# Latent attention in a decoder layer: scaled query rows, a maximum written negated, and one reciprocal for four blocks of sums

## The chip, the cores and the metric

The kernel is one program on one core of a Trainium2 chip. The metric is the device time of one execution in microseconds, the median of the runs. Engines are named as the profile names them: PE is TensorE, DVE is VectorE, ACT is ScalarE, POOL is GpSimd, SP is SyncE, which issues DMAs.

## The reference

One decoder layer on 1024 tokens of width 1024, everything in float32: a latent attention (MLA) and a retention side by side, a gated mix of the two, a cross-attention to 256 memory tokens, a gated MLP with a causal convolution, and a final norm. The change lies in the latent attention alone: 8 heads, 96 columns for each query and key (64 plain, 32 rotary), 64 for each value.

```python
q = (rms_norm(c_q, g_q_lat[l]) @ w_uq[l]).reshape(B, S, MLA_HEADS, MLA_NOPE + MLA_ROPE)
q_nope, q_rope = q[..., :MLA_NOPE], rotary(q[..., MLA_NOPE:], positions)
...
o_a = causal_block_attention(q_full, k_full, v_a.transpose(0, 2, 1, 3),
                             (MLA_NOPE + MLA_ROPE) ** -0.5)
...
def one(args):                       # one block of 128 queries
    s = jnp.einsum('bhqd,bhkd->bhqk', q_blk, k).astype(jnp.float32) * scale
    s = jnp.where(kpos[None, :] <= qpos[:, None], s, neg)
    p = jax.nn.softmax(s, axis=-1).astype(v.dtype)
    return jnp.einsum('bhqk,bhkd->bhqd', p, v)
```

## The kernel before

The five engines run streams of their own, written out by hand in one function, and are tied together by counting semaphores only. An engine works through its stream in order: an instruction that waits holds up all that stand behind it on its engine. Products keep float32 accuracy by splitting each operand into a high and a low part and adding three products (`mm3`: high·high, high·low, low·high, lines 336, 341 and 342). So each tile that TensorE reads is made twice: ScalarE copies the high part out of PSUM (line 878), and VectorE subtracts it to get the low part (line 1378, `lo`). Names ending in `h` and `l` are these parts.

The program starts with memory rows, rotary angles and the transposed input. VectorE's first instructions copy constants (line 1386), turn the positions into floats (`posf`, 1387) and multiply them to angles (`ang`, 1401). Behind that come the retention, the gates, the latents, and then the attention.

**The latents.** TensorE sums the squares of the query latents over columns (line 550, semaphore `l_ss`) and those of the key latents (554). ScalarE takes the square root of the first sums into `lrq` (line 1092: 16 columns, two for each of the 8 row tiles) and of the second into `lr` (1095). Before a function that is not loaded, the compiler puts a table load. VectorE inverts `lrq` (1624) and `lr` (1626). The rows of the queries come out of PSUM multiplied by `lrq` into `qrow` (1104).

**The attention.** For each of the 8 heads the 8 blocks of 128 queries are walked in the order 1, 3, 2, 0, 5, 7, 6, 4 (`QORDER`). Block i has (i + 1) · 128 keys, so its rows of scores are 128 to 1024 columns long. I call a block by that number i. Four blocks in a row are a group: 1, 3, 2, 0 fill one half of the output columns, with at most 512 keys, and 5, 7, 6, 4 the other. The code counts the blocks by w (0 to 63) and the groups by g (0 to 15). For a block:

- TensorE makes the scores in PSUM, masks the diagonal block (629) and signals `m_s`. It is two blocks ahead.
- VectorE takes the row maximum into `amax` (1692) and multiplies it by minus the scale into `aneg` (1695), each one column per block, and waits for itself between the two.
- ScalarE takes the exponential of the scale times the score plus `aneg` into `prow` (1149), and with it the sum of the row into one column of `asum`.
- TensorE transposes `prow` in pieces of up to four 128-wide tiles (641); ScalarE and VectorE make `p0h`/`p0l` (first kind of group) or `p1h`/`p1l` (second kind) of them. The pieces alternate between two banks of PSUM, so a transpose waits until the `lo` of the piece two before is done (`m_ptl`).
- VectorE inverts the sum of the row into one column of `ainv` (1711, `m_inv`, semaphore `m_ri`).

Behind a group stand its value matmuls (662: 12 for the first kind, 24 for the second), then TensorE spreads the four columns of `ainv` by transposes against a broadcast (675), ScalarE copies these to `oT` (1133), and VectorE multiplies the value sums by them (1720). Between the blocks of a head the keys and queries of the next head are made (`aux`: transposes of query rows at 607 and key matmuls; the parts are called `kbh`/`kbl` and `mqh`/`mql`). In the last head this is absent, and the splitting of finished outputs (`oth` on ScalarE, `otl` on VectorE) takes its places.

VectorE's order within block w is: the output of the group before last's end (only second block of a group), the low parts of block w, a low part of the next head if one is due, the maximum of block w + 2 and its `aneg`, then the reciprocal of block w + 1. ScalarE's is: the high parts of block w, the exponential of block w + 1, a high part of the next head. TensorE's is: transposes of block w, next head's piece, scores of block w + 2, and behind the first block of a group the value matmuls of the group before.

## Time and profile before

| | us |
|---|---|
| median of 3 runs | 2019.67 (2018.27 to 2021.47) |
| profiled execution, its own time | 2023.43 |
| span in that profile, first to last instruction | 2021.70 |
| mean granted TensorE clock | 0.977 of full speed |
| busy in the span: TensorE / VectorE / GpSimd / ScalarE | 1913.7 / 929.2 / 850.0 / 555.2 |

The profile is one execution taken by the hardware profiler. Times count from the first instruction. [...] The chain of waits goes back from the last instruction, at each step to what released it, or to the instruction before it on its engine; a piece there is only the part of an instruction that lies on the chain. "issue" is time in which the engine waited for nothing that the profile shows. Rows of the instruction timeline give the whole duration, and in brackets the idle time before and what ended it. Small instructions of one engine overlap in these rows, as the next begins while the last one finishes. The attention runs from about 645 to 852 us.

### The profile page before, as it was taken

To read this page: it belongs to the slowest core of one execution; us is meant where nothing else is said; L and a number is where in the kernel's file an instruction comes from. 1 tells how busy PE (TensorE), PEld (TensorE's weight loads), DVE (VectorE), ACT (ScalarE), POOL (GpSimd) and SP (SyncE) were. 2 spreads that over 40 slices of the span, in tenths; PEclk is the share of its full clock that TensorE was granted. 3 is DMA by queue.
4 is the path that set the end of the run, shared out by engine and by line. 5 is a ranking of instruction groups with operands and counts; after the bars stand their busy time and mean duration, and the time that the engine had idled before them with its cause. 6 is when DMAs were issued, how large, how long until landed. Compare 5 with 4: busy or idle time off the path is not lost.

```text
span 2021.7 us, 25216 instructions
## 1 busy us (share of the span) xinstructions
PE 1913.7 (95%) x9196; PEld 1590.4 (79%) x9196; DVE 929.2 (46%) x1518; ACT 555.2 (27%) x976; POOL 850.0 (42%) x324
## 2 busy tenths in 40 slices
PE   7999999999997888889999999999999999999997
PEld 6788888888875777667878878887888788878876
DVE  4345454000116666645345443665157515542664
ACT  6322223100024555531133221322022102210234
POOL 5733333466642000224533334455645565565461
PEclk9999999999987999989999999999999999999998
DMA  6510111223311000143221222111211121112112
GB/s 244 191 42 25 38 31 52 94 94 96 101 32 32 1 1 1 63 165 127 94 73 63 62 75 82 42 52 52 63 53 42 53 71 42 52 53 63 52 52 83
DMA packets 42203, 136.79 MB, mean 68 GB/s; under 512 B 4240, under 2 KB 10512, under 8 KB 41616
## 3 DMA queue, kind: packets, MB, share of 16 engines
q1 hardware_dynamic: 29072, 93.77, 14.8%
q10 hardware_dynamic: 13056, 41.95, 5.5%
q8 instruction: 55, 0.90, 0.2%
q14 instruction: 20, 0.16, 0.0%
HBM read 114.73 MB, written 20.97 MB: 67 GB/s over the span
## 4 chain that ended last, share of the span: by engine, by line
PE 82%; DVE 8%; ACT 4%; issue 2%; DMA 2%; POOL 1%; ACTq 0%; DVEq 0%; SPq 0%; POOLq 0%
PE ps L336 25%; PE ps L341 25%; PE ps L342 25%; PE ps L662 3%; ACT prow L1149 1%; PE ps L641 1%; DVE p1l L1378 1%; DVE t L1381 1%; DVE yb L1902 1%; DMA raw<-in_slabs 1%; DVE amax L1692 1%; PE ps L455 0%; DVE kbl L1378 0%; DVE sab L1755 0%; ACT oT L878 0%
## 5 line engine op out<-in xcount | busy, mean ns | idle before, releaser
L320 POOL TENSOR_SCALAR wh<-raw 128x1024 fp32r<-128x1024 f32 x152 | 428.1, 2816 | 1091.4 <-PE ps L336 905.8
L322 POOL TENSOR_TENSOR wl<-raw,wh 128x1024 fp32r<-128x1024 f32 x152 | 381.2, 2508 | 12.7
L336 PE MATMUL ps<-uh,wh 128*128 128x512 f32 (+1 forms) x576 | 229.5, 398 | 2.4 <-POOL wl L322 2.4
L342 PE MATMUL ps<-uh,wl 128*128 128x512 f32 (+1 forms) x576 | 226.4, 393 | 0.0
L341 PE MATMUL ps<-ul,wh 128*128 128x512 f32 (+1 forms) x576 | 226.2, 393 | 0.0
L336 PE MATMUL ps<-fah,wh 128*128 128x512 f32 x352 | 139.4, 396 | 6.1 <-DVE fal L1378 5.1
L336 PE MATMUL ps<-f0h,wh 128*128 128x512 f32 x352 | 137.0, 389 | 1.3 <-DVE z L1886 1.3
L342 PE MATMUL ps<-fah,wl 128*128 128x512 f32 x352 | 138.0, 392 | 0.0
L341 PE MATMUL ps<-fal,wh 128*128 128x512 f32 x352 | 137.9, 392 | 0.0
L336 PE MATMUL ps<-f1h,wh 128*128 128x512 f32 x352 | 137.1, 390 | 0.3 <-DVE f1l L1381 0.3
L342 PE MATMUL ps<-f1h,wl 128*128 128x512 f32 x352 | 136.9, 389 | 0.0
L341 PE MATMUL ps<-f0l,wh 128*128 128x512 f32 x352 | 136.9, 389 | 0.0
L342 PE MATMUL ps<-f0h,wl 128*128 128x512 f32 x352 | 136.9, 389 | 0.0
L341 PE MATMUL ps<-f1l,wh 128*128 128x512 f32 x352 | 136.9, 389 | 0.0
L336 PEld LDWEIGHTS ps<-uh,wh 128*128 128x128 f32 (+1 forms) x576 | 108.3, 188 | 25.8 <-POOL wl L322 2.6
L342 PEld LDWEIGHTS ps<-uh,wl 128*128 128x128 f32 (+1 forms) x576 | 107.9, 187 | 24.9
L341 PEld LDWEIGHTS ps<-ul,wh 128*128 128x128 f32 (+1 forms) x576 | 108.3, 188 | 23.3
L1333 ACT ACTIVATE ya<-z,sm 128x512 f32<-128x512 f32 x44 | 35.9, 817 | 301.4 <-DVE z L1886 301.4
L1381 DVE SCALAR_TENSOR_TENSOR ya<-z,sm,ya 128x512 f32<-128x512 f32 x88 | 87.9, 999 | 53.8 <-ACT ya L1333 49.9
L1920 DVE TENSOR_TENSOR hF<-ps,hF 128x512 f32 x48 | 33.2, 692 | 144.3 <-PE ps L342 144.0
L1886 DVE TENSOR_TENSOR z<-ps,rbF 128x512 f32<-128x512 f32 x88 | 60.8, 691 | 71.6 <-PE ps L342 67.7
L1608 DVE TENSOR_TENSOR mxr<-ps,sig 128x512 f32<-128x512 f32 x16 | 11.1, 692 | 177.9 <-PE ps L342 177.9
(352 smaller groups left out, 4081.9 us busy)
## 6 DMA issues: line engine op xcount, KB each, us to landing
raw<-in_slabs SPq DMA_DIRECT2D x160, 512.0 KB, 3.6
rawk<-in_slabs SPq DMA_DIRECT2D x4, 1024.0 KB, 9.7
xs<-in_x SPq DMA_DIRECT2D x8, 512.0 KB, 10.5
s_ga<-sig ACTq DMA_DIRECT2D x8, 512.0 KB, 2.6
s_mr<-mxr ACTq DMA_DIRECT2D x8, 512.0 KB, 5.0
xtile<-in_x ACTq DMA_DIRECT2D x8, 512.0 KB, 6.1
sab<-s_ga ACTq DMA_DIRECT2D x8, 512.0 KB, 4.0
mrb<-s_mr ACTq DMA_DIRECT2D x8, 512.0 KB, 5.6
```

The source lines that it names most:

```text
L320: pool.tensor_scalar(wh[:, j, :], raw[:, j % RAWS, :], 1.0, None, ALU.mult).then_inc(S["w_hi"], 1)
L322: pool.tensor_tensor(wl[:, j, :], raw[:, j % RAWS, :], wh[:, j, :].bitcast(f32), ALU.subtract).then_inc(S["w_ready"], 1)
L336: l = pe.matmul(o, lh, rh, start=start, stop=False)
L341: pe.matmul(o, lh, rl, start=False, stop=False)
L342: return pe.matmul(o, ll, rh, start=False, stop=stop)
L641: l = pe.transpose(ps[:, 6 + q % 2, (c % CH) * P:(c % CH + 1) * P], prow[:, w % 2, c * P:(c + 1) * P], ident)
L662: return pe.matmul(ps[:, 1, qs], vv[:, c, v], pp[:, c, qs], start=start, stop=stop, skip_group_check=True)
L1149: act.activation(prow[:, w % 2, 0:n], s2(w)[:, 0:n], ACT.Exp, scale=QK ** -0.5, bias=aneg[:, 0, w % 4:w % 4 + 1], accum_out=asum[:, 0, w % ...
L1333: act.activation(y[:, half(b)], z[:, 2 + b * H2:2 + (b + 1) * H2], ACT.Identity, scale=smc("cw2", c + FB * x_), bias=smc("b_conv", c + FB ...
L1381: return dve.scalar_tensor_tensor(out=o, in0=a, scalar=s_, in1=b_, op0=op0, op1=op1)
L1886: dve.tensor_tensor(z[:, 2 + b * H2:2 + (b + 1) * H2], ps[:, b, :], rbF[:, b, :], ALU.mult).then_inc(d_free[b], 1)
L1920: dve.tensor_tensor(hb, ps[:, b, :], hb, ALU.add).then_inc(d_free[b], 1)
```

## The change

- The query rows carry the scale of the scores. `lrq` is the square root of (sum of squares / 256 + eps); it becomes the square root of 96 times that, by another `scale` and by a bias `epsq` = 96 · eps. Its inverse is the norm's factor times 96^-0.5, and `qrow` is multiplied by it as before. The exponential has no scale any more. `epsq` is a new column, made by VectorE at the start, and ScalarE waits for it before the square root.
- The row maximum goes straight into `aneg`, by a reduction whose result is negated. `amax`, the multiplication and the semaphore `m_mx` between the two are gone.
- The reciprocal is taken once for a group: 128 × 4 instead of four of 128 × 1, behind the maximum that follows the low parts of the group's last block. The sums use both halves of `asum` in turn, so the exponential of the first block of a group waits for the reciprocal of two groups before. TensorE's wait at the transposes of `ainv` counts groups instead of blocks.
- `epsq` takes its column from the padding (80 to 79), so every other tile stays where it was.

```diff
--- before.py
+++ after.py
@@ -148,8 +148,9 @@
         rst_x = sb("rst_x", [P, NT])
         rsm = sb("rsm", [P, NT, 2])
         mst = sb("mst", [P, 3, MB])
+        epsq = sb("epsq", [P, 1])
         amax, aneg, asum, ainv = (sb(n, [P, 2, CH]) for n in ("amax", "aneg", "asum", "ainv"))
-        sb("line_up_tiles", [P, 80])
+        sb("line_up_tiles", [P, 79])
         ps = ctx.enter_context(nc.psum_tensor("ps", [P, 8, H2], f32))
 
 
@@ -256,7 +257,7 @@
                      "r_hi r_lo y_t gn_st var std yn_done yT_t yg_done y_hi y_lo "
                      "g_st0 g_st1 ld_k0 ld_k1 ld_k2 ld_k3 "
                      "l_e l_ss l_std l_rc l_c l_hi l_lo k_row k_r1 k_r2 k_T k_hi k_lo "
-                     "q_r1 q_rope v_evh o_hi o_lo aux_t aux_hi aux_lo m_s m_mx m_neg m_exp m_ptt m_pth m_ptl "
+                     "q_r1 q_rope v_evh o_hi o_lo aux_t aux_hi aux_lo m_s m_neg m_exp m_ptt m_pth m_ptl "
                      "m_pv m_ri sa_ld0 sa_ld1 mr_ld0 mr_ld1 mix_m mix_hi mix_lo "
                      "o_gh o_gl o_sq o_ac o_z ac_h ac_l ss_t ss_s rb_r rb_t rb_c g1_h g1_l h_sp "
                      "xq_h xq_l mm_ld mm_sq mm_st mm_rc mm_n mm_t mm_hi mm_lo kv_h v_done mv_h mv_l kv_sp k_ld v_ld "
@@ -668,7 +669,7 @@
                         one(c, n)
                 one(0, 2, stop=True).then_inc(S["m_pv"], 1)
 
-                pe.wait_ge(S["m_ri"], CH * (g + 1))
+                pe.wait_ge(S["m_ri"], g + 1)
                 pe.wait_ge(S["aux_lo"], USE_OF["sum", g])
                 for j in range(CH):
                     t = UNITS[CH * g + j][1] % CH
@@ -1088,9 +1089,10 @@
                         act.activation(lsq[:, half(b)], ps[:, b, :], ACT.Square).then_inc(d_free[b], 1)
                     else:
                         copy(zkr[:, half(b)], ps[0:ROPE, b, :]).then_inc(d_free[b], 1)
+            act.wait_ge(S["cst"], 5)
             act.wait_ge(S["l_ss"], 1)
             act.activation(lrq[:, :, :], ps[:, 2, 0:2 * NT].rearrange("p (t c) -> p t c", c=2), ACT.Sqrt,
-                           scale=1.0 / QR, bias=cnc("eps")).then_inc(S["l_std"], 1)
+                           scale=float(QK) / QR, bias=epsq[:, :]).then_inc(S["l_std"], 1)
             act.wait_ge(S["l_ss"], 2)
             act.activation(lr[:, :], ps[:, 4:6, :].rearrange("p a n -> p (a n)"), ACT.Sqrt, scale=1.0 / KVR,
                            bias=cnc("eps")).then_inc(S["l_std"], 1)
@@ -1144,10 +1146,13 @@
             def m_exp(w):
                 n = (UNITS[w][1] + 1) * P
                 act.wait_ge(S["m_neg"], w + 1)
+                if w % CH == 0:
+                    at_least(act, S["m_ri"], w // CH - 1)
                 if w >= 2:
                     act.wait_ge(S["m_ptt"], PIECE0[w - 1])
-                act.activation(prow[:, w % 2, 0:n], s2(w)[:, 0:n], ACT.Exp, scale=QK ** -0.5,
-                               bias=aneg[:, 0, w % 4:w % 4 + 1], accum_out=asum[:, 0, w % 4:w % 4 + 1]).then_inc(S["m_exp"], 1)
+                act.activation(prow[:, w % 2, 0:n], s2(w)[:, 0:n], ACT.Exp,
+                               bias=aneg[:, 0, w % 4:w % 4 + 1],
+                               accum_out=asum[:, w // CH % 2, w % CH:w % CH + 1]).then_inc(S["m_exp"], 1)
 
             def m_pth(w):
                 i, g = UNITS[w][1], w // CH
@@ -1385,6 +1390,7 @@
             for o, n in ((ones_r, "ones"), (ident_r, "ident"), (mask_r, "mask")):
                 dve.tensor_copy(o[:, :], cn[:, CN0[n]:CN0[n] + P]).then_inc(S["cst"], 1)
             dve.tensor_copy(posf[:, :], posi[:, :]).then_inc(S["cst"], 1)
+            dve.tensor_scalar(epsq[:, :], cnc("eps"), float(QK), None, ALU.mult).then_inc(S["cst"], 1)
 
             inv = cn[:, CN0["inv"]:CN0["inv"] + NF]
 
@@ -1394,7 +1400,7 @@
             def angle(n):
 
                 if n == 0:
-                    dve.wait_ge(S["cst"], 4)
+                    dve.wait_ge(S["cst"], 5)
                 else:
                     dve.wait_ge(S["angs"], n)
                 if n == 0:
@@ -1688,12 +1694,9 @@
                 n = (UNITS[w][1] + 1) * P
                 c = 2 + 2 * (w % 2)
                 dve.wait_ge(S["m_s"], w + 1)
-                at_least(dve, S["m_exp"], w - 1)
-                dve.tensor_reduce(amax[:, 0, w % 4:w % 4 + 1], ps[:, c:c + 2, :].rearrange("p a n -> p (a n)")[:, 0:n], AX.X,
-                                  ALU.max).then_inc(S["m_mx"], 1)
-                dve.wait_ge(S["m_mx"], w + 1)
-                dve.tensor_scalar(aneg[:, 0, w % 4:w % 4 + 1], amax[:, 0, w % 4:w % 4 + 1], -QK ** -0.5, None, ALU.mult).then_inc(
-                    S["m_neg"], 1)
+                at_least(dve, S["m_exp"], w - 3)
+                dve.tensor_reduce(aneg[:, 0, w % 4:w % 4 + 1], ps[:, c:c + 2, :].rearrange("p a n -> p (a n)")[:, 0:n], AX.X,
+                                  ALU.max, negate=True).then_inc(S["m_neg"], 1)
 
             def m_ptl(w):
                 i, g = UNITS[w][1], w // CH
@@ -1706,10 +1709,9 @@
                        ps[:, 6 + q % 2, 0:(c1 - c0) * P].rearrange("p (a n) -> p a n", n=P),
                        (p1h if g % 2 else p0h)[at]).then_inc(S["m_ptl"], 1)
 
-            def m_inv(w):
-                dve.wait_ge(S["m_exp"], w + 1)
-                dve.reciprocal(ainv[:, w // CH % 2, w % CH:w % CH + 1], asum[:, 0, w % CH:w % CH + 1]).then_inc(
-                    S["m_ri"], 1)
+            def m_inv(g):
+                dve.wait_ge(S["m_exp"], CH * (g + 1))
+                dve.reciprocal(ainv[:, g % 2, :], asum[:, g % 2, :]).then_inc(S["m_ri"], 1)
 
             def m_out(g):
                 h, b = divmod(g, 2)
@@ -1723,7 +1725,6 @@
             NW = len(UNITS)
             m_max(0)
             m_max(1)
-            m_inv(0)
             for w in range(NW):
                 h, r = divmod(w, NT)
                 if w > CH and w % CH == 1:
@@ -1733,8 +1734,8 @@
                     aux_lo(h + 1, AUX_AT[r])
                 if w + 2 < NW:
                     m_max(w + 2)
-                if w + 1 < NW:
-                    m_inv(w + 1)
+                if w % CH == CH - 1:
+                    m_inv(w // CH)
                 if h == MH - 1 and r < 4:
                     o_lo(r // 2, r % 2)
                 if h == MH - 1 and r >= 6:
```

What this does to VectorE around block 5, in the first head. Before: the key part `kbl`, the three small instructions of block 5 (its maximum, `aneg`, the inverse of block 0), the low part of block 0 (`p0l`), the next `kbl`, and the same for block 7.

```order
L1378 TENSOR_TENSOR kbl<-ps,kbh 64x512
L1692 TENSOR_REDUCE amax<-ps 128x1
L1695 TENSOR_SCALAR aneg<-amax 128x1
L1711 RECIPROCAL ainv<-asum 128x1
L1378 TENSOR_TENSOR p0l<-ps,p0h 128x128
L1378 TENSOR_TENSOR kbl<-ps,kbh 64x512
L1692 TENSOR_REDUCE amax<-ps 128x1
L1695 TENSOR_SCALAR aneg<-amax 128x1
L1711 RECIPROCAL ainv<-asum 128x1
L1378 TENSOR_TENSOR p1l<-ps,p1h 128x4x128
```

The same place in the changed kernel, from the same `kbl` to block 5's first `p1l`.

```order
L1383 TENSOR_TENSOR kbl<-ps,kbh 64x512
L1698 TENSOR_REDUCE aneg<-ps 128x1
L1383 TENSOR_TENSOR p0l<-ps,p0h 128x128
L1383 TENSOR_TENSOR kbl<-ps,kbh 64x512
L1698 TENSOR_REDUCE aneg<-ps 128x1
L1714 RECIPROCAL ainv<-asum 128x4
L1383 TENSOR_TENSOR p1l<-ps,p1h 128x4x128
```

Block 5's maximum is now followed at once by `p0l`, and block 7's by the reciprocal of the whole first group.

VectorE at the end of a head, from the last query part `mql` on: the maximum of the next head's block 1, the low parts of block 4 (`p1l`, two pieces), the maximum of the next head's block 3, the low part of its block 1 (`p0l`). Before:

```order
L1378 TENSOR_TENSOR mql<-ps,mqh 96x512
L1692 TENSOR_REDUCE amax<-ps 128x1
L1695 TENSOR_SCALAR aneg<-amax 128x1
L1711 RECIPROCAL ainv<-asum 128x1
L1378 TENSOR_TENSOR p1l<-ps,p1h 128x4x128
L1378 TENSOR_TENSOR p1l<-ps,p1h 128x128
L1692 TENSOR_REDUCE amax<-ps 128x1
L1695 TENSOR_SCALAR aneg<-amax 128x1
L1711 RECIPROCAL ainv<-asum 128x1
L1378 TENSOR_TENSOR p0l<-ps,p0h 128x2x128
```

And in the changed kernel:

```order
L1383 TENSOR_TENSOR mql<-ps,mqh 96x512
L1698 TENSOR_REDUCE aneg<-ps 128x1
L1383 TENSOR_TENSOR p1l<-ps,p1h 128x4x128
L1383 TENSOR_TENSOR p1l<-ps,p1h 128x128
L1698 TENSOR_REDUCE aneg<-ps 128x1
L1714 RECIPROCAL ainv<-asum 128x4
L1383 TENSOR_TENSOR p0l<-ps,p0h 128x2x128
```

Nothing stands between the first maximum and `p1l` any more.

ScalarE at the square root of the query latents, with what each instruction waits for. `zkr` is the last copy of the latents, and the table load brings the square root. Before:

```order
L878 ACTIVATE zkr<-ps 32x512 [waits done0]
L878 ACTIVATE zkr<-ps 32x512 [waits done1]
L1092 ACT_TABLE_LOAD
L1092 ACTIVATE lrq<-ps,cn 128x16 [waits l_ss]
L1095 ACTIVATE lr<-ps,cn 128x1024 [waits l_ss]
L878 ACTIVATE qrow<-ps,lrq 128x384 [waits done0,l_rc]
```

And in the changed kernel:

```order
L879 ACTIVATE zkr<-ps 32x512 [waits done0]
L879 ACTIVATE zkr<-ps 32x512 [waits done1]
L1094 ACT_TABLE_LOAD [waits l_ss]
L1094 ACTIVATE lrq<-ps,epsq 128x16 [waits cst]
L1097 ACTIVATE lr<-ps,cn 128x1024 [waits l_ss]
L879 ACTIVATE qrow<-ps,lrq 128x384 [waits done0,l_rc]
```

The root now has two waits, and the one for TensorE's sums (`l_ss`) stands ahead of the table load, which waited for nothing before.

## Rows read from the trace of the kernel before

**Rows 1.** The page: shares of the chain that ended last, by engine.
```profile
PE 82%; DVE 8%; ACT 4%; issue 2%; DMA 2%; POOL 1%; ACTq 0%; DVEq 0%; SPq 0%; POOLq 0%
```

**Rows 2.** The attention: length, busy PE, PEld, DVE, ACT, POOL; clock, DMA share, GB/s.
```profile
645.00:852.00 207.00, 175.99 (x1058) 147.65 (x1057) 137.52 (x336) 117.79 (x274) 10.27 (x4) 0.97 0.03 7
```

**Rows 3.** The instructions of lines 1695 and 1711: ns min/median/max, first and last start.
```profile
L1695 DVE TENSOR_SCALAR aneg<-amax x64: 153/154/155, 644.9 to 847.0; 128x1 f32<-128x1 f32 x64
L1711 DVE RECIPROCAL ainv<-asum x64: 151/153/164, 646.4 to 848.8; 128x1 f32<-128x1 f32 x64
```

**Rows 4.** Waits in the attention, 645 to 852: us in total, times, longest.
```profile
PE ps L641 <- DVE p1l L1378: 18.7, 23, 1.6
...
ACT prow L1149 <- DVE aneg L1695: 13.2, 22, 0.9
```

**Rows 5.** The chain through one head, 697 to 724: start us, us, what.
```profile
697.01 4.65 PE ps L662 x24
...
706.56 0.95 DVE amax L1692
...
707.53 0.17 DVE aneg L1695
...
707.72 0.99 ACT prow L1149 x2
...
721.00 0.42 DVE amax L1692
...
721.45 0.08 DVE aneg L1695
721.53 0.14 DVE ainv L1711
721.67 0.60 DVE p1l L1378
```

**Rows 6.** The chain in the other heads: first and last of each place.
```profile
655.29 0.16 DVE aneg L1695
...
668.91 0.15 DVE ainv L1711
...
826.21 0.14 DVE ainv L1711
...
837.72 0.17 DVE aneg L1695
```

**Rows 7.** Timeline of that head: PE at `kbl`, then DVE and ACT around `p1l`.
```profile
709.97 0.64 PE L607 MATMUL ps<-cn,qrow 128*96 128x128 f32 x4 [0.20 <-DVE kbl L1378]
...
720.39 0.69 DVE L1378 TENSOR_TENSOR mql<-ps,mqh 96x512 fp32r<-96x512 f32 x1 [0.48 <-ACT mqh L878]
...
721.59 0.67 DVE L1378 TENSOR_TENSOR p1l<-ps,p1h 128x512 fp32r<-128x512 f32 x1
...
721.64 0.47 ACT L1149 ACTIVATE prow<-ps,aneg 128x256 f32<-128x256 f32 x1 [0.18 <-DVE aneg L1695]
```

**Rows 8.** Timeline of the last head: `oth` on ACT, `otl` on DVE.
```profile
834.82 0.63 ACT L878 ACTIVATE oth<-oT 128x512 fp32r<-128x512 f32 x1
...
835.62 0.68 DVE L1378 TENSOR_TENSOR otl<-oT,oth 128x512 fp32r<-128x512 f32 x1
```

**Rows 9.** Timeline of ACT at the square roots of the latents.
```profile
591.51 1.28 ACT L1092 ACT_TABLE_LOAD   x1
595.29 0.27 ACT L1092 ACTIVATE lrq<-ps,cn 128x16 f32<-128x16 f32 x1 [2.50 <-PE ps L550]
598.91 1.11 ACT L1095 ACTIVATE lr<-ps,cn 128x1024 f32<-128x1024 f32 x1 [3.35 <-PE ps L554]
```

**Rows 10.** Timeline of DVE at the start.
```profile
7.78 0.83 DVE L1401 TENSOR_TENSOR ang<-posf,cn 128x640 f32<-128x640 f32 x1
```

**Rows 11.** Behind the last block: the window 850 to 855, then the chain.
```profile
850.00:855.00 5.00, 3.66 (x9) 2.92 (x10) 1.52 (x4) 1.05 (x3) 0.00 (x0) 0.50 0.76 279
...
851.34 7.08 PE ps L662 x24
```

## The prediction

> **What bounds the kernel now.** I read the page first. Of the chain that ended last TensorE has 82%, VectorE 8%, ScalarE 4% [rows 1]. So VectorE and ScalarE matter only where TensorE waits for them. The change touches the causal attention of the eight heads, which runs from about 645 us to 852 us. There TensorE is busy for 176.0 of 207.0 us, VectorE for 137.5, ScalarE for 117.8 [rows 2]: no engine is full, and the time is set by a chain that goes from one engine to the next. One head takes some 26 us.
>
> The three instructions that the change is about are, for each of the 64 query blocks, the row maximum, its product with minus the scale (154 ns) and one reciprocal (153 ns) [rows 3]. Added up the last two are 64 × 0.154 + 64 × 0.153 = 19.6 us of VectorE. The waits in this stretch show ScalarE waiting for `aneg` 22 times, 13.2 us, and TensorE waiting for VectorE's `p1l` 23 times, 18.7 us [rows 4]. Neither figure is a gain: each is the whole wait, of which the small instructions are the last part. What counts is where they lie on the chain.
>
> The chain through one head [rows 5] goes: the 24 value matmuls of the head before (4.65 us); copies; the maximum of block 5 on VectorE (0.95), then `aneg` (0.17 beside 0.02 of issue), then block 5's exponential. From there a key copy leads to TensorE, whose scores and value matmuls run without a gap. It comes back to VectorE with the maximum of the next head's block 1 (0.42), then `aneg` (0.08) and `ainv` (0.14), then `p1l` of block 4, which frees the PSUM bank that TensorE's next transposes need. Those lead straight into the next 24 value matmuls. So of eight `aneg` and eight `ainv` in a head, two and one are on the chain. The other heads repeat it: block 5's `aneg` is on the chain 8 times, once a head from 655.29 to 837.72, and the pair before `p1l` 7 times, with `ainv` from 668.91 to 826.21 [rows 6].
>
> **The change, part by part.**
>
> *`aneg` of block 5 goes.* The maximum ends at 707.51 and the exponential starts at 707.72 [rows 5]. With the maximum written negated the exponential can start 0.02 us after it: 0.19 us earlier, 8 times, 1.52 us. Next late is the key copy behind it, `kbl` and TensorE's transposes of the queries, and these move by the same 0.19, since TensorE waits 0.20 us for that `kbl` [rows 7].
>
> *`aneg` and `ainv` of the next block 1 go.* The maximum ends at 721.42 [rows 5], `p1l` starts at 721.59 [rows 7]. Two VectorE instructions without a wait between them overlap by 0.08: `mql` runs 720.39 to 721.08 [rows 7], the maximum starts at 721.00. So `p1l` could start at 721.34, 0.25 earlier. The exponential of block 1 must be there as well: it waited 0.18 us for `aneg` [rows 7], gains that, and then its ScalarE predecessor is what is late. Gain for TensorE between 0.18 and 0.25; I take 0.25, also what the chain counts (721.42 to 721.67), since in the chain `p1l` comes last. Seven times: 1.75 us (bounds 1.3 to 1.8). [...]
>
> *The last head* has no next head to prepare. `otl` stands there between `ainv` and block 2's `p0l`. It starts at 835.62 behind `ainv` and needs `oth`, which ends at 834.82 + 0.63 = 835.45 [rows 8]; so it gains about 0.14, and half of that is lost again, because `p0l` then waits for its copy. I take 0.07 (bounds 0 and 0.25) on top of the 0.19 of `aneg` already counted.
>
> *The reciprocals, one of 4 columns for every four blocks.* 64 become 16. They wait for the last exponential of the group, which is done when they are reached, as `p1l`/`p0l` of that block comes before them on VectorE and needs it too. Who needs them is TensorE, only behind the 12 or 24 value matmuls of the group (24 take 4.65 us), and these start later than the reciprocal, since one more block's scores stand before them. So the value matmuls hide the later inversion; without them it would cost its 0.15 us. No reciprocal of four columns stands in the trace of the attention; the nearest is that of 16 columns, `lrq`, and that of one, 0.153 [rows 3]. It now stands behind the maximum of block 7 and behind that of the next head's block 3, and neither place is on the chain: block 7's `p1l` ends under TensorE's value matmuls. Cost 0, bounds 0 and 16 × 0.16 = 2.6 us.
>
> *New waits.* ScalarE's exponential of every first block of a group also waits for the reciprocal of two groups back, done a whole group (some 10 us) before. It stands as a wait ahead of the one for `aneg`, so the sequencer is through with it while it waits. Cost 0; if it were not, 0.02 to 0.1 us each for blocks 5 and 1, at most 1.6 us.
>
> *The query scale.* The square root of the 16 columns now has another scale and bias and the same shape: 0. But it waits for two semaphores now, and the table load ahead of it (1.28 us at 591.51, done while ScalarE waited) is issued only behind the wait for the sums [rows 9]. It starts at about 595.3 instead, and the root at 596.6. Behind it ScalarE waits until 598.91 for TensorE's second sum, 3.35 us idle [rows 9], and only later come the query rows that use the scale. Hidden, 2.3 us to spare; with that cover gone it would cost 1.28.
>
> *`epsq`* is one tiny instruction (about 0.15 us) ahead of `ang` [rows 10], in the opening stretch in which VectorE runs without a gap and TensorE has not yet begun. Small instructions that don't depend on each other start 0.08 apart, as `aneg` and `ainv` do (721.45 and 721.53). Cost 0.07 us (bounds 0 and 0.15).
>
> Sum: −1.52 − 1.75 − 0.07 + 0.07 = −3.3 us. The profiled execution took 2023.43 us (span 2021.70) and would take 2020.1. The median of the three runs is 2019.67; nothing in the sum depends on the difference, so the forecast is **2016.4 us**. With the bounds of the parts on the chain: −2.6 to −3.6; with 1.6 us for the new ScalarE waits on top −1.0, and with all 16 reciprocals on the chain too +1.6. For these two no row puts them on the chain, so they widen the range to one side only.
>
> **The rivals.**
>
> 1. *More than the chain says.* If taking 19.6 us off VectorE helped wherever an engine waited for it: 22 × 0.19 + 7 × 0.25 = 5.9 us, 2013.8. For it: 22 waits for `aneg` [rows 4]. Against: most of these exponentials are followed by a transpose that then waits for something else, and the chain passes two of them a head.
>
> [...]
>
> 3. *Nothing gained.* If a negated maximum took 0.15 us more than a plain one, the same as the instruction it replaces, only the `ainv` part stays: about 2019.0.
>
> 4. *Slower: the negated maximum is a second pass over the row.* Then the two maxima on the chain double: 0.95 + 0.42 = 1.37 us a head against 0.44 gained, +0.93 × 8 = 7.4 us, 2027. It breaks even where a maximum grows by a third, and is measurably slower where it grows by two thirds. No row shows a negated reduce. [...]
>
> That the change does not do what it says is excluded by the built order: the product and 48 reciprocals are gone.
>
> **How the numbers follow.** Forecast (2015.2 to 2017.6) 0.60; more than the chain 0.10; a dip less 0.08; a dip more 0.12; nothing gained 0.05; slower 0.05. A measurement of this kernel can tell about 0.2% (4.0 us) from no change. Faster by over 0.2% means under 2015.6: rival 1, the dip less and the lower edge of the forecast (0.12): 0.30. Slower 0.05. Within 0.2%: 0.65. The range takes in the dips, a part of the new waits, the greater part of rival 1 and the bounds of the sum: 2013.5 to 2019.5; left out are "slower" and parts of rivals 1 and 3.
>
> **What would show it.** The maximum unchanged in duration by shape (0.95 for 768 columns, 0.42 for 256); the exponential of block 5 starting 0.02 us behind it; `p1l` of block 4 starting inside the end of the maximum before it; a head 0.44 us shorter; the stage 3.3 us shorter, everything behind it shifted as a whole; the table load at the square root exposed but nothing late behind it. Wrong would be: a longer maximum, a head shorter by much more than 0.44 (rival 1), TensorE waiting at the reciprocal's transposes, or a stage that is shorter while the span is not (the clock).

## The result: 38 us slower, and the long matmuls start 6 ns further apart

| | before | changed |
|---|---|---|
| median of 4 runs, us | 2018.97 (2017.88 to 2021.47) | 2057.03 (2053.64 to 2058.61) |
| ratio, with 95% interval | | 1.0186 [1.0173, 1.0199] |
| span of the profiled execution, us | 2021.7 | 2051.9 |
| mean granted clock in it | 0.977 | 0.981 |

The forecast was 2016.4 us, in a range of 2013.5 to 2019.5. Everything it said of the attention happened, somewhat more strongly, and was worth 4 to 5 us. Beside it stands a loss of some 40 us which none of its steps had.

The chain of the changed kernel, by engine (the line that answers to [rows 1]):

```profile
PE 84%; DVE 8%; ACT 4%; issue 3%; DMA 1%; ACTq 0%; DVEq 0%; SPq 0%
```

Two points more for TensorE. Its busy time rose from 1913.7 to 1944.5 us with the same 9196 matmuls, and VectorE's fell from 929.2 to 907.3. So the loss is TensorE's and not a wait. Cut at the attention's first transposes and at its end, the two traces differ by +8.4 us before the attention, −5.1 in it, and +26.9 behind it, where the change touches nothing. The loss is spread over all that TensorE does densely. A stretch of plain weight products shows it. Groups by line and shape, 400 to 500 us (columns: count, busy us, mean ns of one, idle before), first of before, then of the changed kernel:

```profile
L342 PE MATMUL ps<-uh,wl 128*128 128x512 f32 x108 | 42.0, 389 | 0.0
```

```profile
L343 PE MATMUL ps<-uh,wl 128*128 128x512 f32 x112 | 44.2, 395 | 0.0
```

389 ns have become 395, and the same holds for the two other products of `mm3`. Matmuls overlap in the trace (each lasts 0.39 to 0.40 us and the next starts 0.22 to 0.24 behind it in the rows below), so what they cost is the distance from start to start. The timeline of TensorE there (start us, duration us), before and then changed:

```profile
440.16 0.39 PE L336 MATMUL ps<-uh,wh 128*128 128x512 f32 x1
440.39 0.39 PE L341 MATMUL ps<-ul,wh 128*128 128x512 f32 x1
440.61 0.39 PE L342 MATMUL ps<-uh,wl 128*128 128x512 f32 x1
...
445.60 0.39 PE L336 MATMUL ps<-yth,wh 128*128 128x512 f32 x1
```

```profile
439.85 0.40 PE L337 MATMUL ps<-uh,wh 128*128 128x512 f32 x1
440.08 0.39 PE L342 MATMUL ps<-ul,wh 128*128 128x512 f32 x1
440.32 0.40 PE L343 MATMUL ps<-uh,wl 128*128 128x512 f32 x1
...
445.45 0.40 PE L337 MATMUL ps<-uh,wh 128*128 128x512 f32 x1
```

Two steps take 0.45 us before and 0.47 after. The rows round to 0.01 us, so the size is read over more of them: from the first to the last row shown are 24 steps in both traces, 5.44 us before and 5.60 after, which is 226.7 ns and 233.3 ns a step. The starts as the traces hold them, in whole ns, give the same means from 400 to 500 us (441 and 428 steps). Both stretches are at a granted clock of 1.00 (the share of full speed that a trace gives for TensorE; the traces of the layer's kernels hold two values of it, 1.00 and 0.50). In the whole trace 6,709 matmuls of 128x512 before and 6,718 after are followed by another within 260 ns at that clock. Their mean distance is 227.22 ns before and 233.07 after, so 6,700 × 5.85 ns = 39 us. That is the size of the loss. In a row as `ps<-uh,wl`, I call the operand of 128x512 (`uh`) the moving one and that of 128x128 (`wl`) the stationary one.

The same instructions, the same shapes, the same clock: what differs is the data's place in SBUF. The new column `epsq` is one float wide. In the built programs it takes 32 bytes all the same: it stands at byte 63040 of each partition, and `aneg` behind it is at 63104 where it was at 63072. The padding went from 80 to 79 columns, which is 316 bytes instead of 320, and still fills 320: it starts at 63200, and the next tile stands at 63520. So the column was not paid for by the padding: every tile behind it moved up by 32 bytes (`uh` from byte 63488 to 63520), while the weights `wh` (25088), `wl` (41472) and the constants stand ahead of it and stayed. Matmuls with both operands in moved tiles lost little or nothing: `vrl` with `p1h` kept its 227 ns, while the few with `vrh` beside it went from a median of 227 to 230 and 232, for which I have no reason. So the suspicion is the place of the moving operand (the activations) against that of the stationary one (the weights).

### The profile page after: what moved, and what is told of

It is laid out like the page before. It is cut to its first block, busy times and chain, and to the rows that moved or that the text cites. A ratio compares the mean times of both kernels' runs of the same rounds, so it can differ in the third digit from the quotient of the medians.

```text
span 2051.9 us, 25104 instructions
## 1 busy us (share of the span) xinstructions
PE 1944.5 (95%) x9196; PEld 1582.0 (77%) x9196; DVE 907.3 (44%) x1407; ACT 555.1 (27%) x976; POOL 852.0 (42%) x324
## 4 chain that ended last, share of the span: by engine, by line
PE 84%; DVE 8%; ACT 4%; issue 3%; DMA 1%; ACTq 0%; DVEq 0%; SPq 0%
PE ps L337 26%; PE ps L342 25%; PE ps L343 25%; PE ps L663 3%; PE ps L642 1%; ACT prow L1153 1%; DVE p1l L1383 1%; DVE t L1386 1%; DVE yb L1903 1%; PE ps L456 0%; DVE sab L1756 0%; ACT oT L879 0%; DVE kbl L1383 0%; DMA xtile<-in_x 0%; DVE hF L1765 0%
## 5 line engine op out<-in xcount | busy, mean ns | idle before, releaser
L337 PEld LDWEIGHTS ps<-fah,wh 128*128 128x128 f32 x352 | 66.2, 188 | 33.6 <-issue 9.4
```

What stands on the lines that cost most here:

```text
L337: l = pe.matmul(o, lh, rh, start=start, stop=False)
```

## Experiments on the place of the tiles

Each kernel was timed against runs of the kernel before on the same chip.

**1. The changed kernel with its tiles put back.** `uh` is at 63488 again; all else is the change (lines left out of an edit are marked `...`).

```diff
         epsq = sb("epsq", [P, 1])
...
-        sb("line_up_tiles", [P, 79])
+        sb("line_up_tiles", [P, 72])
```

> The changed kernel with the padding in front of the large tiles cut from 79 to 72 columns, so that every large tile stands at the address that it had in the kernel before (epsq takes 32 bytes, not 4). Theory 'place' (the 32 bytes by which all large tiles had slid make each 128x512 matmul take 233.3 instead of 226.7 ns): matmul to matmul 226.7 ns again, and what is left is the change in the attention, -3.3 us against the kernel before, about 2016, bounds -2.6 to -3.6. Rival 'instructions' (the negated maximum, the new waits or the scale slow TensorE down): still about 2057, +38.

Measured: 2015.26 us, ratio 0.9974 [0.9953, 0.9995]. The distance between matmuls is 226.7 ns again (here and in the experiments on this kernel that follow, the mean from 400 to 500 us, where nothing else is said). Seven columns of padding, which are 32 bytes in the built program as 79 take the room of 80, take the whole loss away. The same text, timed again against more runs:

> The changed kernel with its tiles put back, the same text as before under a new label, to narrow its interval: 2012.4 to 2015.3 us, ratio 0.9965 to 0.9975 (five microseconds for 8 x 0.58 us of the heads). The rival 'the whole change is worth less than the negation alone' would show as a ratio above 0.998.

Measured: 2014.82 us, ratio 0.9974 [0.9964, 0.9985].

**2. The kernel before with only its tiles moved up by 32 bytes.** No other change.

```diff
-        sb("line_up_tiles", [P, 80])
+        sb("line_up_tiles", [P, 88])
```

> The kernel before with 8 columns more of padding: all large tiles 32 bytes up, weights and constants where they were, no other change. 'Place': 5,600 matmuls of 512 columns x 6.7 ns = +37 us, with the rest up to +41: about 2058. 'Instructions': 2019, no change.

Measured: 2057.63 us, ratio 1.0181 [1.0153, 1.0209], 233.3 ns. The place alone makes the loss. With experiment 1 this settles its cause: it appears without the change and disappears with it in.

**3. The weights moved up by 32 bytes, the tiles left.** The raw slabs and the constants, which lie beside the weights, move with them. If only the address of the moving operand mattered, this would cost nothing.

```diff
-        sb("line_up_slabs", [P, 96])
+        sb("line_up_slabs", [P, 104])
...
-        sb("line_up_tiles", [P, 80])
+        sb("line_up_tiles", [P, 72])
```

> The kernel before with the raw slabs, the weights and the constants 32 bytes up and the large tiles where they were. In the dense stages the weights are the stationary operand. Theory 'apart' (what counts is whether the moving and the stationary operand start at the same place within 64 bytes): slow as the changed kernel, +37 to +41, matmul to matmul 233.3. Rival 'moving' (only the moving operand's own address counts): dense stages unchanged at 226.7, and only the few matmuls that read weights as the moving operand (value rows of the memory, query and value rows of the attention, a few hundred) slower, +1 to +3 us.

Measured: 2057.16 us, ratio 1.0181 [1.0147, 1.0216], 233.3 ns.

**4. Both moved up by 32 bytes.**

```diff
-        sb("line_up_slabs", [P, 96])
+        sb("line_up_slabs", [P, 104])
```

> The kernel before with everything 32 bytes up, weights and large tiles alike. 'Apart': both operands move together, 226.7 ns, no change, 2019. 'Moving': every matmul reads its moving operand from an address 32 past a multiple of 64: +37 to +43 us, about 2058.

Measured: 2019.11 us, ratio 0.9993 [0.9977, 1.0008], 226.7 ns. Experiments 2 to 4 together: neither operand has to be where it was before. It is their places against each other that count. The product `uh` with `wl`, groups of 400 to 500 us, in experiments 1, 2, 3 and 4:

```profile
L343 PE MATMUL ps<-uh,wl 128*128 128x512 f32 x108 | 42.1, 390 | 0.0
L342 PE MATMUL ps<-uh,wl 128*128 128x512 f32 x109 | 43.1, 395 | 0.0
L342 PE MATMUL ps<-uh,wl 128*128 128x512 f32 x110 | 43.5, 396 | 0.0
L342 PE MATMUL ps<-uh,wl 128*128 128x512 f32 x108 | 42.1, 389 | 0.0
```

**5. How round? The tiles moved up by 64 bytes.**

```diff
-        sb("line_up_tiles", [P, 80])
+        sb("line_up_tiles", [P, 96])
```

> The kernel before, its tiles 64 bytes further up (so they lie at other places modulo 128, 256 and 512 bytes, but still at 0 modulo 64, as the weights do). Theory 'a step of 64': only the place modulo 64 counts; matmuls of 128x512 start every 226.7 ns, the time is that of the kernel before, within 2 us. Rival 'a wider step' (128 to 512 bytes): the time between starts rises as it did with 32 bytes, to 233 ns, and the kernel takes some 37 us more, 2057. Half of that would be a step per pair of tiles.

Measured: 2034.80 us, ratio 1.0073 [1.0059, 1.0088]. "A step of 64" was my theory, and it fell. The mean distance over the whole trace is 229.2 ns; 6,700 × 1.95 ns = 13 us of the 15. Not all matmuls pay the same. By the starts in ns of this trace `f0h` with `wh` takes 230.5 and `f0h` with `wl` 227.7. The groups of 400 to 500 us, where the duration shows it too:

```profile
L341 PE MATMUL ps<-ul,wh 128*128 128x512 f32 x107 | 41.9, 392 | 0.0
L342 PE MATMUL ps<-uh,wl 128*128 128x512 f32 x106 | 41.8, 394 | 0.0
L336 PE MATMUL ps<-uh,wh 128*128 128x512 f32 x106 | 41.1, 388 | 0.0
```

**6. Matmuls alone.** 21 batches with nothing beside them, the layer left out, to see whether other traffic is needed, and a first table.

```diff
+            for i, (n, m, s) in enumerate(PAIRS):
+                for r in range(REP):
+                    l = pe.matmul(ps[:, i % 8, :], sta[i][:, s + r % 4 * P:s + r % 4 * P + P] if s + r % 4 * P + P <= 544 else sta[i][:, s:s + P],
+                                  mov[i][:, m:m + H2], start=r == 0, stop=r == REP - 1)
```

> Leaves the layer out entirely: 21 batches of 32 matmuls of 128x512, nothing else beside them, each batch with its own moving tile (mov..) and stationary tile (sta..). The start of the moving columns lies 0 to 512 bytes, that of the stationary 0 to 128 bytes, behind a place that is 0 modulo 64. Theory 'apart': 226.7 ns from start to start where the two starts are equal modulo 64 bytes (aa, ae, ag, ah, ai, bc, be, ca, cb, cc, cd, da), 233.3 where they are 32 bytes apart (ac, bb, ce, cf: cf is 8 floats and ce 16 floats apart, so ce is equal modulo 64), and unknown for 16 and 48 bytes (ab, ad). The rival 'only beside other traffic': all batches at one rate, because without VectorE, ScalarE and DMAs in SBUF nothing collides. A second rival, 'it is the output or the fp32 rate': all batches at one rate as well, but another than 226.7.

Measured: no batch needs traffic beside it, since both levels appear with only TensorE at work. But which batch has which was half wrong: of the twelve expected fast, five were. Groups by tile, slow ones and then fast ones (`da` repeats the first pair, `aa`, whose first six steps took 426 to 594 ns each):

```profile
L151 PE MATMUL ps<-movbd,stabd 128*128 128x512 f32 x32 | 7.7, 396 | 0.0
L151 PE MATMUL ps<-movae,staae 128*128 128x512 f32 x32 | 7.6, 397 | 0.0
...
L151 PE MATMUL ps<-movda,stada 128*128 128x512 f32 x32 | 7.5, 390 | 0.0
L151 PE MATMUL ps<-movba,staba 128*128 128x512 f32 x32 | 7.4, 389 | 0.0
L151 PE MATMUL ps<-movbe,stabe 128*128 128x512 f32 x32 | 7.4, 389 | 0.0
```

`ae` was expected fast and is slow; `bd`, whose two starts are 96 bytes apart, is slow. The tiles' own starts were not all equal modulo 512, and with the true addresses `ae` is a moving operand at 64 against a stationary one at 0, and `be` 0 against 256. That asked for a full table.

**7. A table of places.** 13 by 13 pairs, 40 matmuls each, again without the layer.

```diff
+        mov = [placed("mov%03d" % o, o, 2048) for o in OFFS]
+        sta = [placed("sta%03d" % o, o, 1024) for o in OFFS]
```

> Leaves the layer out entirely. Matmuls of 128x512 alone, 13 moving tiles by 13 stationary tiles, 40 matmuls a pair; the number in a tile's name is the place of its first byte modulo 512. The rule of 64 has fallen with the tiles 64 bytes up (+15 us) and with the first table of matmuls. Theory 'place modulo 512, relative': 226.7 ns a matmul where both numbers are equal (mov000/sta000, mov064/sta064, mov032/sta032), 233.3 for mov032/sta000 and mov000/sta032 (the two cases of the slow kernels), 226.7 for mov000/sta256 (seen once), between 226.7 and 233.3 for mov064/sta000. Rival 'only a moving tile at 0 is fast': the row mov000 fast, the others 233.3, mov032/sta032 too (against it: the kernel with everything 32 bytes up was fast). Rival 'modulo 64': mov000 by sta064, sta128, sta192, sta256, sta384, sta448 all at 226.7.

Measured: the mean distance in ns from start to start, over the 20 steps from the 19th to the 39th of a pair's 40 matmuls, by the starts in ns. Rows are the moving operand's first byte modulo 512, columns the stationary one's (the places of 16, 48 and 144 are left out here):

```
 mov\sta      0     32     64     96    128    192    256    288    384    448
       0  226.7  233.3  233.3  234.2  232.4  229.1  226.7  233.3  231.9  229.0
      32  233.3  226.7  233.3  233.3  234.1  233.4  233.3  226.7  234.2  233.4
      64  233.3  233.3  226.7  233.3  233.3  232.5  229.1  233.3  233.3  232.4
      96  233.4  228.9  233.3  226.7  233.3  234.4  233.4  228.8  233.3  234.1
     128  232.6  233.4  228.9  233.3  226.7  233.3  232.3  233.4  226.7  233.3
     192  233.3  234.1  233.3  233.4  228.8  226.7  233.3  234.1  228.8  226.7
     256  226.7  233.3  233.3  234.1  232.3  229.1  226.7  233.3  231.9  229.1
     288  233.3  226.7  233.3  233.3  234.2  233.4  233.3  226.7  234.2  233.4
     384  232.4  233.4  228.9  233.3  226.7  233.3  232.3  233.4  226.7  233.3
     448  233.3  234.1  233.3  233.4  228.8  226.7  233.3  234.1  228.8  226.7
```

All 18 pairs that lie at multiples of 32 bytes and are equal modulo 256 take 226.7 ns. Of the 148 unequal pairs of the full table 99 take 232 ns or more, 38 lie between, and 11 are as fast as the equal ones; their mean is 232.1. All 11 have an operand at 16, 48 or 144; of the 82 unequal pairs at multiples of 32 none is under 228.7 ns, so there the rule has no exception in this table. The theory "modulo 512" was too strict, "modulo 64" and "only a moving operand at 0" are wrong. At 16, 48 and 144, equal places took 230.0, 233.3 and 233.3 ns. An unequal pair isn't a fixed number either: 0 against 144 took 233.3 here and 226.7 as `ba` in experiment 6, where the sequence, the tiles' absolute addresses and the number of stationary columns walked through were others. The same is seen in experiment 5, whose 64 against 0 is 233.3 in the table and on the mean 229.2 in the kernel. What decides there stays open.

**8. The table's claim, in the kernel: tiles up by 256 bytes.**

```diff
-        sb("line_up_tiles", [P, 80])
+        sb("line_up_tiles", [P, 144])
```

> The kernel before, its tiles 256 bytes further up: moving operands at 256 modulo 512, weights at 0. Theory 'a step of 256 is free' (moving at 0 and stationary at 256 gave 226.7 in the first table): 226.7 ns and the time of the kernel before, within 2 us. Rival 'the two starts must agree modulo 512': between 229 and 233.3 ns as with 64 and 32 bytes, so 2034 to 2057 us.

Measured: 2020.45 us, ratio 1.0002 [0.9992, 1.0011], 226.7 ns. So 256 bytes are free where 64 cost 15 us and 32 cost 37 to 40.

**9. Is the change's own gain there in the slow place as well?** Experiment 2 again, with more runs.

> The kernel before with its tiles 32 bytes up, the same text as before under a new label. The slow place alone gave 1.0181 with a wide interval and the whole change 1.0186, although the change's own gain, about 5 us, should lie between them. If the gain stands in the slow place as in the fast one: 1.0186 / 0.9974 = 1.021, 2062. If something gives the gain back there: 1.0186, 2057.

Measured: 2059.35 us, ratio 1.0199 [1.0185, 1.0213]. The changed kernel's 1.0186 is lower by 0.0013, and the two intervals together leave about ±0.002: both a gain of 5 us (0.0026) and one of nothing fit. The attention itself is shorter in the changed kernel, 209.6 us against 214.7 before, 213.8 in experiment 2 and 214.7 in this repeat. The total doesn't resolve it.

## Experiments on the attention

With the tiles in place, the two halves of the change can be weighed. The measure is a head's period, from the first of its 24 value matmuls to that of the next; in undisturbed heads it repeats within 0.03 us.

**10. The negated maximum alone** (from experiment 1, with one reciprocal per block again; the waits for it on TensorE and ScalarE count blocks again, and the calls stand where they stood before).

```diff
...
-            def m_inv(g):
-                dve.wait_ge(S["m_exp"], CH * (g + 1))
-                dve.reciprocal(ainv[:, g % 2, :], asum[:, g % 2, :]).then_inc(S["m_ri"], 1)
+            def m_inv(w):
+                dve.wait_ge(S["m_exp"], w + 1)
+                dve.reciprocal(ainv[:, w // CH % 2, w % CH:w % CH + 1], asum[:, w // CH % 2, w % CH:w % CH + 1]).then_inc(
+                    S["m_ri"], 1)
...
```

> The changed kernel with its tiles put back, but with one reciprocal per block as before; scale in the query rows and negated maximum stay. Theory by places: block 5's and block 7's exponentials come 0.19 and up to 0.13 us earlier a head, and of the 0.25 us ahead of the low part of block 4 the 0.17 of the product is gained and the 0.08 of the reciprocal is not: a head of 25.7 us, 0.08 to 0.1 longer than with the whole change, 0.45 to 0.5 shorter than before; about 0.7 us behind the whole change in time, too little for a verdict. Rival 'the reciprocals are what counts' (missed third place is theirs): a head of 25.9 or more.

**11. The reciprocal for four alone** (from experiment 1, with the maximum written plain and multiplied by −1 behind it).

```diff
...
-                dve.tensor_reduce(aneg[:, 0, w % 4:w % 4 + 1], ps[:, c:c + 2, :].rearrange("p a n -> p (a n)")[:, 0:n], AX.X,
-                                  ALU.max, negate=True).then_inc(S["m_neg"], 1)
+                dve.tensor_reduce(amax[:, 0, w % 4:w % 4 + 1], ps[:, c:c + 2, :].rearrange("p a n -> p (a n)")[:, 0:n], AX.X,
+                                  ALU.max).then_inc(S["m_mx"], 1)
+                dve.wait_ge(S["m_mx"], w + 1)
+                dve.tensor_scalar(aneg[:, 0, w % 4:w % 4 + 1], amax[:, 0, w % 4:w % 4 + 1], -1.0, None, ALU.mult).then_inc(
+                    S["m_neg"], 1)
```

> The changed kernel with its tiles put back and one reciprocal per group, but the maximum is written plain and multiplied by -1 into aneg as a second instruction. Theory by places: only the 0.08 us of the reciprocal ahead of the low part of block 4 is gained, a head of 26.1 us (26.17 before). Rival 'the reciprocals are what counts': a head of 25.9 or less, since the third place (the transposes of the inverse sums held up by VectorE's queue) is then relieved too.

Measured, with the whole change of experiment 1 beside them:

| | head, us | less than before | time, ratio |
|---|---|---|---|
| before | 26.17 | | |
| reciprocal for four alone | 26.11 | 0.06 | 2016.51, 0.9984 [0.9974, 0.9994] |
| negated maximum alone | 25.66 | 0.51 | 2012.44, 0.9966 [0.9953, 0.9979] |
| both (experiments 1 and its repeat) | 25.60 | 0.57 | 2014.82, 0.9974 [0.9964, 0.9985] |

The two halves add up, and the negated maximum has nine tenths of it. Both came out as the theory by places had them. In total time "negated alone" is ahead of "four alone" by 0.0018 with about ±0.0016, so just; the heads would make it 8 × 0.45 = 3.6 us, or 0.0018. "Negated alone" and "both" can't be ranked: a difference of 7 × 0.06 = 0.4 us is far below their intervals. The place ahead of block 4's `p1l` shows the arithmetic in rows. Timeline of VectorE there, negated alone, then four reciprocals alone, then both:

```profile
717.16 0.41 DVE L1698 TENSOR_REDUCE aneg<-ps 128x1 f32<-128x256 f32 x1
717.49 0.15 DVE L1714 RECIPROCAL ainv<-asum 128x1 f32<-128x1 f32 x1
717.56 0.86 DVE L1383 TENSOR_TENSOR p1l<-ps,p1h 128x512 fp32r<-128x512 f32 x2
```

```profile
719.52 0.41 DVE L1698 TENSOR_REDUCE amax<-ps 128x1 f32<-128x256 f32 x1
719.97 0.15 DVE L1701 TENSOR_SCALAR aneg<-amax 128x1 f32<-128x1 f32 x1
720.04 0.88 DVE L1383 TENSOR_TENSOR p1l<-ps,p1h 128x512 fp32r<-128x512 f32 x2
```

```profile
715.27 0.41 DVE L1698 TENSOR_REDUCE aneg<-ps 128x1 f32<-128x256 f32 x1
715.60 0.88 DVE L1383 TENSOR_TENSOR p1l<-ps,p1h 128x512 fp32r<-128x512 f32 x2
```

From the maximum's start to that of `p1l`: 0.59 before [rows 5, 7], then, in the order shown, 0.40, 0.52 and 0.33. An instruction of one column costs 0.07 where it waits for nothing. The product cost 0.19, for it waited until the maximum was written, and without it the next instruction starts 0.08 inside the maximum's end.

## Why the prediction was wrong, step by step

**The step that failed** is none of the terms of the sum. It is what no term stood for, a cost put at nothing: the description of the change says that "every other tile stays where it was", and the prediction that "the change does not do what it says is excluded by the built order". The built order lists instructions, and those were as said. It does not list addresses. I took 80 = 79 + 1 for an identity of columns; in bytes it is 320 against 32 + 320. The built program says where each tile lies, and one look at `uh` there would have shown it. What it would cost, though, no row of before that I read could tell, as nearly all its matmuls of 512 columns had operands at equal places modulo 256. The case of slower had a chance of 0.05 and another mechanism, and rested on the attention only. Measured: 39 us by 6,700 matmuls; that the place is the cause is shown by experiments 1 to 4.

**`aneg` of block 5: 0.19 a head. Right.** The way from the first `kbl` of the head to the query transposes, which goes by block 5's maximum and exponential before, took 4.02 us (705.95 to 709.97) and takes 3.82 with the tiles back. The chain of experiment 1 (start, us, what):

```profile
700.83 0.69 DVE kbl L1383
...
704.65 0.64 PE ps L608 x4
```

TensorE now runs through here by itself, without the exponential on the chain. Its wait for `kbl` ahead of the transposes was named as "next late". The query transposes, before and in experiment 1 (what TensorE idled for ahead of them: us, times):

```profile
L607 PE MATMUL ps<-cn,qrow x64: 272/273/449, 639.6 to 823.2; 128*96 128x128 f32 x64
its engine sat idle before it (us, times) until:
  DVE kbl L1378: 7.8, 15
```

```profile
L608 PE MATMUL ps<-cn,qrow x64: 272/273/450, 635.7 to 815.2; 128*96 128x128 f32 x64
its engine sat idle before it (us, times) until:
  DVE kbl L1383: 5.2, 8
```

Seven of 15 waits are gone, one of two a head.

**`aneg` and `ainv` ahead of block 4's `p1l`: 0.25 a head. Right**, 0.26 by the rows above. It is 0.19 by the product and 0.07 by the reciprocal. The chain of experiment 1 (start, us, what) now goes from the maximum straight to `p1l` and the transposes, where [rows 5] had two small instructions between:

```profile
715.27 0.41 DVE aneg L1698
715.68 0.62 DVE p1l L1383
716.30 0.14 issue
716.43 0.41 PE ps L642 x2
```

The overlap of 0.08 held (715.68 less 715.60).

**A third place, missed: 0.13 a head.** The heads are shorter by 0.57 to 0.58 and not by 0.44. The difference lies between the query transposes and the copy of the first group's inverses, `oT`: 4.50 us before (709.97 to 714.47), 4.38 in experiment 1 (704.65 to 709.03). Block 7's `aneg` stood ahead of its exponential, and that ahead of `mqh` and `mql`, which free the bank into which TensorE spreads `ainv`. The chain, before and in experiment 1:

```profile
713.87 0.58 PE ps L675 x4
...
714.47 0.60 ACT oT L878
```

```profile
708.56 0.45 PE ps L676 x4
709.03 0.60 ACT oT L879
```

The four small transposes take 0.58 on the chain before and 0.45 after. The chain of before names TensorE alone there, so the wait inside them has to be read from what TensorE idled for, and there it is only "issue":

```profile
L675 PE MATMUL ps<-cn,ainv x64: 270/272/295, 661.6 to 858.6; 128*128 128x128 f32 x64
its engine sat idle before it (us, times) until:
  issue: 1.6, 7
```

Seven times, once a head; with the change these are gone. That experiment 10 has this gain and experiment 11 hasn't (their heads leave no room for it otherwise) shows that it comes from the maximum's side and not from the reciprocals'. The way over `mqh` and `mql` I only argued, from the order of the code; the rows fit it, as `mql` ends 3.70 us behind the start of the query transposes before (713.67) and 3.51 in experiment 1 (708.17).

**The sum.** −3.3 us for the attention was mis-sized by this place: with the tiles back the attention takes 210.5 and 210.8 us instead of 214.7, so −3.9 to −4.2. The whole is −5.2 (2019 less 0.9974 × 2019), with an interval of −7.3 to −3.0, which holds the forecast −3.3 as well. Rival 1 ("more than the chain says", 2013.8) is nearer to the median, though by one more place on the chain and not by 22 waits: ScalarE still waits for `aneg`, in the changed kernel 14 times for 7.4 us where [rows 4] had 22 for 13.2, and most of what it gained reached nobody. The 0.07 us of the last head can't be told: the time from the value matmuls of the seventh head to those of the eighth varies from 23.2 to 23.7 us among the runs with the old attention, in which the granted clock falls to 0.50 at different points, from 3.6 us ahead of the eighth head's value matmuls (experiment 4) to 0.1 us behind their start (experiment 5).

**The negated maximum is no second pass. Right.** Lines 1692 of before and 1698 of the changed kernel, ns min/median/max, and the reciprocal of four columns:

```profile
L1692 DVE TENSOR_REDUCE amax<-ps x64: 273/750/1215, 644.5 to 846.2; 128x1 f32<-128x256 f32 x8, 128x1 f32<-128x512 f32 x8, 128x1 f32<-128x384 f32 x8, 128x1 f32<-128x128 f32 x8
```

```profile
L1698 DVE TENSOR_REDUCE aneg<-ps x64: 271/747/1212, 652.8 to 850.3; 128x1 f32<-128x256 f32 x8, 128x1 f32<-128x512 f32 x8, 128x1 f32<-128x384 f32 x8, 128x1 f32<-128x128 f32 x8
...
L1714 DVE RECIPROCAL ainv<-asum x16: 157/165/168, 666.9 to 855.1; 128x4 f32<-128x4 f32 x16
```

The medians are 750 ns plain and 747 negated. The four-column reciprocal takes 165 ns against 153, and nobody waits for it, as said. The new waits of ScalarE show nowhere: in the traces of the changed kernel and of experiment 1 no idle time of any engine ends at the reciprocal of line 1714. The upper bound of 0.1 us for each of them was my estimate, and no run shows it.

**The square root: hidden, but with less to spare than I said.** ScalarE in the changed kernel, to be read against [rows 9]:

```profile
604.36 1.28 ACT L1094 ACT_TABLE_LOAD   x1 [2.92 <-PE ps L551]
605.65 0.27 ACT L1094 ACTIVATE lrq<-ps,epsq 128x16 f32<-128x16 f32 x1
606.14 1.11 ACT L1097 ACTIVATE lr<-ps,cn 128x1024 f32<-128x1024 f32 x1 [0.21 <-PE ps L555]
608.06 0.58 ACT L879 ACTIVATE qrow<-ps,lrq 128x384 f32<-128x384 f32 x1 [0.81 <-PE ps L343]
```

The load is exposed, as foreseen, and the root of the second sums still waits 0.21 for TensorE. The margin of 2.3 us was that of an execution in which TensorE's granted clock was 0.50 there. The window at the root, before and then changed (length, busy PE, PEld, DVE, ACT, POOL; clock last but two):

```profile
594.00:596.00 2.00, 2.00 (x7) 1.59 (x8) 0.25 (x1) 0.27 (x1) 0.00 (x0) 0.50 0.00 0
```

```profile
604.00:606.00 2.00, 2.00 (x7) 0.79 (x6) 0.04 (x1) 1.56 (x2) 0.00 (x0) 1.00 0.00 0
```

With the clock at 0.50 for most of it, from 593.2 us on, the way from the last `zkr` to `lr` takes 8.0 us before; at 1.00 it takes 5.3. That is the dip less of the chances, worth 2.7 us in this place; at the last 24 value matmuls of before, which start at 0.50, it is 7.08 us [rows 11] less 4.65 [rows 5], 2.4. Experiment 1, which has the same instructions, shows the dip there again (7.9 us from the last `zkr` to `lr`), so I put it down to the execution and not to the change; the changed kernel itself has one trace, and so this isn't shown. The dip is part of why the spans differ by 30 us while the medians differ by 38: the profiled execution of the changed kernel (2053.64) was the fastest of its four, and that of before (2023.43) was over its median.

**`epsq`:** 0.07 was written, 0.05 measured. VectorE at the start, to be read against [rows 10]; from `posf` to `ang` it is 0.25 here and was 0.20 (7.58 to 7.78):

```profile
7.77 0.16 DVE L1392 CAST posf<-posi 128x8 f32<-128x8 int32 x1
7.84 0.14 DVE L1393 TENSOR_SCALAR epsq<-cn 128x1 f32<-128x1 f32 x1
8.02 0.82 DVE L1407 TENSOR_TENSOR ang<-posf,cn 128x640 f32<-128x640 f32 x1
```

Its instruction cost 0.05 us and its 32 bytes cost 39 us.

## What to carry to other kernels

An edit that adds or resizes a tile can move all that stand behind it (by 32 bytes here, for one of 4), and a padding that is trimmed by the same count of elements need not undo that; compare the built addresses of the operands as well as the built instructions. Where TensorE is the bound, keep the moving and the stationary operand of its long matmuls at the same place modulo 256 bytes and at multiples of 32 (226.7 ns a matmul of 128x512 in experiment 7, against 228.7 to 234.5), and if a time changes all over a kernel by one factor, look at the distance of two neighbouring matmuls first. In a chain that hands work from engine to engine, an instruction that waits for the one ahead cost 0.19 us here and one that doesn't 0.07, so it is the dependent small instructions that are worth removing.

## What the runs showed of the hardware that I had not expected

The distance between two matmuls of 128x512 depended here on where their two operands lie against each other: 226.7 ns where their starts are equal modulo 256 bytes and at multiples of 32, 228.7 to 234.5 in the table where they are at multiples of 32 and unequal. It needs no other engine at work: with TensorE alone `da` took 226.7 ns a step and `bd` 234.3 (experiment 6, the last 19 steps of each), and the whole table is of TensorE alone (experiment 7). The table is of float32 matmuls of this one shape, each with a weight load of its own; other shapes and types weren't timed alone. Neither operand's own place decides: with the weights alone moved by 32 bytes the step took 233.3 ns (experiment 3), and with both moved 226.7 (experiment 4). What the two would share, why some unequal pairs at 16, 48 or 144 are as fast as equal ones, and why the same pair differs between two kernels, no run here shows.
